# RWKV stage of a two-block kernel: the next pair's fills and key products moved from VectorE to GpSimd and ScalarE

## What is computed

```
decay = exp(-exp(-softplus(-w_raw) - 0.5))
a     = sigmoid(rw_a0 + xa @ rw_a2)
kk    = k * rw_kk, scaled to unit length over each head
k_eff = k * (1 + (a - 1) * rw_ka)
```

```
s = s * w_t + (-(s @ kk_t)) outer (kk_t * a_t) + v_t outer k_t
y_t = s @ r_t
```

## Time and profile before

| | |
|---|---|
| median of 3 runs | 3578.41 us (3572.24 to 3578.68) |
| profiled execution, its own time | 3575.68 us |
| its span | 3574.2 us |
| TensorE matmul busy | 3090.4 us (86%) |
| VectorE busy | 1488.6 us (42%) |
| ScalarE busy | 984.2 us (28%) |
| GpSimd busy | 45.5 us (1%) |

### The profile page before, as it was taken

One profiled execution on the slowest core, in us unless ns is written; L12 is line 12 of the kernel. 1 busy time (PEld: TensorE's weight loads), 2 busy tenths in 40 slices (PEclk: granted clock), 3 DMA queues, 4 the chain that ended last, 5 costly groups with the idle time before them and its releaser, 6 DMA issues. The chain is left out here.

```text
span 3574.2 us, 54419 instructions
## 1 busy us (share of the span) xinstructions
PE 3090.4 (86%) x23420; PEld 1656.0 (46%) x23420; DVE 1488.6 (42%) x3056; ACT 984.2 (28%) x1912; POOL 45.5 (1%) x65
## 2 busy tenths in 40 slices
PE   7888888887799999789995977787999899985996
PEld 3455555555655555444443322334454545542332
DVE  3677777776457567510023100003333424233122
ACT  2344344333124654510011000003324242410001
POOL 0000000000000000000000000000000000000000
PEclk9999999998799999889997999998999999996998
DMA  4212222211311221243056999982211111026997
GB/s 176 67 55 70 80 66 84 83 62 43 112 52 65 80 80 68 100 159 118 0 201 246 421 421 421 421 342 105 111 41 74 47 66 41 15 92 275 426 426 309
DMA packets 118062, 546.90 MB, mean 153 GB/s; under 512 B 32208, under 2 KB 35008, under 8 KB 82496
## 3 DMA queue, kind: packets, MB, share of 16 engines
q1 hardware_dynamic: 111776, 524.69, 38.0%
q0 software_dynamic: 3456, 12.58, 0.9%
q10 hardware_dynamic: 2592, 6.16, 0.4%
HBM read 511.74 MB, written 31.65 MB: 152 GB/s over the span
## 5 line engine op out<-in xcount | busy, mean ns | idle before, releaser
L2349 PE MATMUL mh_ps<-mh_w_ahead,xmT 128*128 128x512 f32 x768 | 336.4, 593 | 0.0
L2084 PE MATMUL ex_ps<-ex_ring,ex_xs 128*64 128x512 f32 x896 | 244.3, 634 | 53.3 <-DMA ex_ring<-expert_slabs_in 42.2
L501 PE MATMUL rw_ps<-hT,rw_w 128*128 128x512 f32 (+1 forms) x640 | 273.9, 555 | 6.6 <-PEq L63 5.8
L2349 PEld LDWEIGHTS mh_ps<-mh_w_ahead,xmT 128*128 128x128 f32 x768 | 144.7, 190 | 167.1 <-issue 165.1
L2084 PEld LDWEIGHTS ex_ps<-ex_ring,ex_xs 128*64 128x64 f32 x896 | 81.6, 146 | 205.7 <-issue 203.3
L1300 PE MATMUL sg_ps<-hTp,sg_w 128*128 128x512 f32 x384 | 171.0, 599 | 0.0
L501 PEld LDWEIGHTS rw_ps<-hT,rw_w 128*128 128x128 f32 x640 | 114.7, 198 | 86.7 <-issue 76.0
L2333 PE MATMUL mh_ps<-xmT,mh_w_ahead 128*128 128x512 f32 x256 | 124.5, 620 | 14.9 <-PEq L63 8.6
L2168 DVE TENSOR_TENSOR ex_hid<-ex_hid,ex_ps 128x512 f32<-128x512 f32 x16 | 11.0, 687 | 288.0 <-PE ex_ps L2084 288.0
L2992 PE MATMUL ge_ps<-ge_ring,ge_xs 128*64 128x512 f32 x512 | 116.0, 606 | 2.8 <-DVE ge_xs L3096 2.8
L1826 PE MATMUL se_ps<-se_w,se_mT 128*128 128x512 f32 x256 | 113.7, 601 | 5.1 <-DMA se_w<-w_out_in 5.1
(11 more groups left out here) (617 smaller groups left out, 5113.6 us busy)
## 6 DMA issues: line engine op xcount, KB each, us to landing
ex_ring<-expert_slabs_in SPq DMA_DIRECT2D x148, 1024.0 KB, 26.7
ge_ring<-expert_slabs_in SPq DMA_DIRECT2D x50, 2048.0 KB, 15.8
mh_w_ahead<-head_slabs_in SPq DMA_DIRECT2D x16, 2048.0 KB, 8.0
rw_mod_w<-mod_w_in SPq DMA_DIRECT2D x64, 384.0 KB, 4.1
ex_first<-expert_slabs_in SPq DMA_DIRECT2D x22, 1024.0 KB, 26.0
rw_mod_w<-ada_in SPq DMA_DIRECT2D x64, 256.0 KB, 3.3
sg_kern<-cum_dram SPq DMA_DIRECT2D x64, 256.0 KB, 3.2
ex_ring<-expert_slabs_in SPq DMA_DIRECT2D x7, 2048.0 KB, 13.8
```

The costliest lines, as they stand in the source:

```text
L501: mm = pe.matmul(where[j, part], w[:, k, P * j:P * j + P], tokens, start=k == 0, stop=k == KC - 1)
L2084: mm = pe.matmul(ps[halves[j], bank, :], src[:, k, halves[j]], home(g + j)[0][:, k, :], start=k == 0, stop=k == KC - 1)
L2349: mm = pe.matmul(ps[:, 4 + t, :], xmT[:, k, P * t:P * t + P], w[:, slot, k, :], start=k == 0, stop=k == KC - 1)
```

## The change

ScalarE computes the key factor `1 + (a - 1) * ka` as `a * ka + (1 - ka)` (`past_gate`, one 128x768 activation per direction) into the storage of `xb` and `low`, which `substitute` has finished with; a 128x1 VectorE instruction prepares `1 - ka`. GpSimd multiplies both by `k` and sums them (`replaced_keys`, two products of 128x768 and a sum of 128x512), then does `fill` for both directions, four products of 128x768 (with `kk * a` now among them) and one of 128x512 each, and only then clears `diag`'s padding and `xb`. `write_keys` and `fill` leave VectorE. `exponents(p, 1)` is cut into three pieces, which stand between scan steps 1, 2, 3 and 4. ScalarE's scaling of the values moves ahead of the second direction's factors.

```diff
+        past_ka = sb("rw_past_ka", [P, 1])
+        keyed = [a.rearrange("p i c -> p (i c)")[:, 0:NT] for a in (xb, low)]
...
-                for c in range(PAIRS):
+                def replaced_keys(p):
+                    pool.wait_ge(s.affine, 2 * p + 2)
+                    pool.wait_ge(s.shifted_k, p + 1)
+                    for d in range(2):
+                        pool.tensor_tensor(keyed[d], keyed[d], kc[:, :], ALU.mult).then_inc(s.keyed, 1)
+                    pool.wait_ge(s.keyed, 2 * p + 2)
+                    if p:
+                        pool.wait_ge(s.bonus_done, p)
+                    pool.tensor_tensor(ksum[:, :], keyed[0][:, CTX:NT], keyed[1][:, CTX:NT], ALU.add).then_inc(s.key_summed, 1)
...
+                def fill(p, d):
+                    rf, bf, kf = (e1, qq, ee) if d == 0 else (e1, ee, qq)
+                    u = of_dir(d)
+                    ul = slice(RW_NCH * d + RW_CC, RW_NCH * d + RW_NCH)
+                    pool.wait_ge(s.factors, 2 * p + d + 1)
+                    if p:
+                        pool.wait_ge(s.mr_kept, 6 * (p - 1) + 3 * d + 3)
+                    pool.tensor_tensor(bk[:, u, 64:P], token_cut(keyed[d]), token_cut(bf[:, :]), ALU.mult)
+                    pool.wait_ge(s.shifted_r, p + 1)
+                    pool.tensor_tensor(kr[:, ul, 64:P], token_cut(rc[:, :]), token_cut(rf[:, :], RW_CC), ALU.mult)
+                    pool.wait_ge(s.kk_done, p + 1)
+                    pool.tensor_tensor(sgs[:, d, :], kk[:, :], aas[:, d, :], ALU.mult).then_inc(s.gated_keys, 1)
+                    pool.tensor_tensor(kr[:, u, 0:64], token_cut(kk[:, :]), token_cut(kf[:, :]), ALU.mult)
+                    pool.wait_ge(s.gated_keys, 2 * p + d + 1)
+                    pool.tensor_tensor(bk[:, u, 0:64], token_cut(sgs[:, d, :]), token_cut(bf[:, :]), ALU.mult).then_inc(s.filled, 1)
+
+                for p in range(PAIRS):
+                    replaced_keys(p)
+                    fill(p, 0)
+                    fill(p, 1)
+                    clear(p)
...
+                def past_gate(p):
+                    par = pars2[:, p % 2, :]
+                    act.wait_ge(s.gates, 4 * p + 4)
+                    for d in range(2):
+                        act.activation(keyed[d], aas[:, d, :], ACT.Identity, scale=par[:, KA:KA + 1], bias=past_ka[:, 0:1]).then_inc(s.affine, 1)
...
+                    if prep:
+                        past_gate(p)
+                    if core:
                         keep_wu(c, 0)
...
+                        centre(p, 2, 0, vc[:, CTX:NT], ps[:, 1, :])
                         factors(p, 1)
                         act.activation(half[:, :, :], half[:, :, :], ACT.Exp, scale=-KAPPA).then_inc(s.halved, 1)
-                        centre(p, 2, 0, vc[:, CTX:NT], ps[:, 1, :])
...
+                    if part == 0:
+                        dve.wait_ge(s.gates, 4 * p + d + 1)
+                        if d:
+                            dve.wait_ge(s.filled, 2 * p + 1)
...
-                        dve.wait_ge(s.kk_done, p + 1)
-                        write_keys(p, 0)
                     if core:
                         keep_mr(c, 3)
-                        dve.wait_ge(s.mr_kept, 6 * c + 4)
-                    if prep:
-                        fill(p, 0)
-                        dve.wait_ge(s.filled, 2 * p + 1)
-                    if core:
                         keep_mr(c, 4)
-                    if prep:
-                        exponents(p, 1)
-                    if core:
                         keep_mr(c, 5)
...
                         scan_step(c, 1)
-                        scan_step(c, 2)
-                    if prep:
-                        write_keys(p, 1)
+                    for part in range(3):
+                        if prep:
+                            exponents(p, 1, part)
+                        if core:
+                            scan_step(c, part + 2)
                     if core:
-                        for step in range(3, 6):
-                            scan_step(c, step)
+                        scan_step(c, 5)
...
-                    if prep:
-                        fill(p, 1)
-                    if core:
                         dve.wait_ge(s.y_done, c + 1)
...
-                        dve.wait_ge(s.filled, 2 * p + 2)
                         dve.wait_ge(s.halved, p + 1)
+                        dve.wait_ge(s.key_summed, p + 1)
```

More of the change, by code:

```diff
@@ L964, in neighbours, with exponents @@
                     link(dve.scalar_tensor_tensor(dst[:, 0:n - 1], u[:, 1:n], par[:, 2 * j + 1:2 * j + 2], dst[:, 0:n - 1], ALU.mult, ALU.add))
-                def exponents(p, d):
-                    dve.wait_ge(s.gates, 4 * p + d + 1)
+                def exponents(p, d, part):
                     sg = sgs[:, d, :]
-                    link(dve.tensor_tensor_scan(qq[:, :], cst("chunk_start"), sg, 0.0, ALU.mult, ALU.add))
                     q3 = qq[:, :].rearrange("p (c t) -> p c t", t=RW_C)
-                    link(dve.tensor_scalar(half[:, d, :], q3[:, :, RW_C - 1], 0.5, None, ALU.mult))
-                    link(dve.tensor_tensor(q3, q3, free_copies(half[:, d, :], RW_C), ALU.subtract))
-                    dve.tensor_tensor(ee[:, :], qq[:, :], sg, ALU.subtract).then_inc(s.exponents, 1)
@@ L975, in write_keys @@
[L975 to L980, removed]
-                    link(dve.scalar_tensor_tensor(aa, aa, 1.0, kc[:, :], ALU.add, ALU.mult))
-                    if d == 0:
-                        dve.tensor_copy(ksum[:, :], aa[:, CTX:NT]).then_inc(s.ksum_started, 1)
-                    else:
-                        dve.wait_ge(s.ksum_started, p + 1)
-                        link(dve.tensor_tensor(ksum[:, :], ksum[:, :], aa[:, CTX:NT], ALU.add))
@@ L988, in fill @@
[L988 to L997 removed]
+                    if part == 0:
+                        dve.wait_ge(s.gates, 4 * p + d + 1)
+                        if d:
+                            dve.wait_ge(s.filled, 2 * p + 1)
+                        link(dve.tensor_tensor_scan(qq[:, :], cst("chunk_start"), sg, 0.0, ALU.mult, ALU.add))
+                    elif part == 1:
+                        link(dve.tensor_scalar(half[:, d, :], q3[:, :, RW_C - 1], 0.5, None, ALU.mult))
+                        link(dve.tensor_tensor(q3, q3, free_copies(half[:, d, :], RW_C), ALU.subtract))
+                    else:
+                        dve.tensor_tensor(ee[:, :], qq[:, :], sg, ALU.subtract).then_inc(s.exponents, 1)
@@ L1028, in _ @@
                         dve.sem_inc(s.shifted_k, 1)
-                        exponents(p, 0)
+                        for part in range(3):
+                            exponents(p, 0, part)
                     if core:
```

12 lines of the change are left out of this document (2 added, 10 removed).

## The result

The changed kernel takes **3534.03 us** (median of 4 runs, 3529.86 to 3537.26) against 3578.55 us (3572.24 to 3583.22) for the kernel before: a ratio of 0.9876, 95% interval 0.9857 to 0.9895. That is 44.5 us less, where 31 against the profiled execution (33.5 against this median) was forecast; 3545 was 11 us too high, and the range 3529 to 3563 holds it. The profiled execution took 3534.92 us, 40.8 less than the one before.

A forecast was written before the change was run, and what follows sets the result against it. The prediction took TensorE to bound the kernel, each wait that goes being nearly its own length off the time. Terms -27.2 - 8.5 + 1.4 + 0 + 3.2 = -31.1 against 3575.7 gave 3545 us, range 3529 to 3563.

The forecast's parts named there:

- Part 1: VectorE's prep work leaves the gap before `mr(4)` and `mr(5)`; both TensorE wait groups go, 14.4 + 12.8 = -27.2 us.
- Part 3: ScalarE's two extra activations ahead of `keep_wu(0)` start it 0.2 us late in seven pairs: +1.4 us.
- Part 2: In the scan, TensorE's 1.21 us wait at step 4 goes in seven pairs, fitting barely: -8.5 us.
- Part 4: The fills on GpSimd stay hidden in the pairs, the second behind ScalarE's copies: 0 us.
- x: Time of a 128x768 two-input product on GpSimd, absent from the trace and taken as 1.75 us.
- between 1 and 2 us: Sign of a right forecast: how long `near(1)` would wait for GpSimd.
- The limit: Longest GpSimd 128x768 product, 2.06 us, at which the second fill still ends before ScalarE takes up direction 1.
- Part 5: The opening turn, without core work to hide behind: second fill 4.6 later, partly hidden by 1.3 us slack, +3.2 us.
- The clock: Rival: TensorE's clock fall may go (5 us won) or come later, up to 1.5 us a pair: 3555 us, chance 0.09.
- a slower GpSimd: Rival: GpSimd's product takes about 2.4 us, costing 11 us in seven pairs and 6 in the opening: 3562 us, chance 0.13.
- the fill as bound: Rival: at 3.1 us a product the second fill makes `near(1)` 4.9 us late per pair: 3592 us, chance 0.05.
- Scan steps beside GpSimd's products: Rival: VectorE's scan steps wait for GpSimd's product under way, 6 us a pair, 43 in all: 3588 us, chance 0.04.

The follow-up runs named there:

- the values' neighbours: The changed kernel plus the second direction's exponents earlier and the values' neighbour instructions standing singly between scan steps; 3526.69 us, ratio 0.9846.

## Why the prediction was right, and what it missed

**Part 1** (-27.2) had the mechanism and too small a size. In a pair without a fall of the clock the two waits of the earlier trace rows are 4.45, and 0.29 more is won because the first matmuls of `mr(4)` now start among those of `wu(5)` instead of behind a wait: 4.74, which is 33 in seven. (`wu(0)` to `crossed_y` is 4.94 shorter in the table: 0.28 of Part 3 comes off the 4.74, and 0.48 is time that TensorE loses inside `new_part` in this one pair of before; the others lose 0.1 to 0.35 there.) The step that failed: "This is a sum over the stage and not one pair's 4.45 times seven, since in some pairs the second wait was shorter." It was shorter, 0.98 to 1.58 in place of 2.40, in the five pairs in which TensorE ran at its lower clock up to it, and there the time was lost all the same. The sum also holds the last pair's 1.04, which has no prep ahead of it and stayed.

**Part 2** (-8.5) held. 1.98 between `crossed_y` and `near(1)`, less the 0.69 that `keys(0)` gives back to ScalarE, is 1.29 a pair against 1.21. It fitted barely, as said: one block of 3.9 us in place of pieces brought the wait back.

**Part 3** (+1.4): `keep_wu(0)` starts 1.42 us behind `wu(0)` instead of 1.14, so 0.28 a pair, 0.18 of it a wait of TensorE. Right.

**Part 4** (0): x is 1.81 (taken 1.75), and `near(1)`'s wait 0.77 (1.3 expected, and "between 1 and 2 us" among the signs, which did not come). The limit was put at 2.06. With the change ScalarE takes up direction 1 at 338.41, 2.0 us behind the end of `near(1)` at 336.40, and one extra product of 1.9 still fitted; the limit is nearer to 1.81 + 2.0 / 4.67 = 2.24. That ScalarE's copies are the cover was shown twice, by the added products and by the one moved forward.

**Part 5** (+3.2) was 5.0. The slack that was to hide 1.3 of it did not: TensorE was idle for 4.4 us ahead of the first `near(1)` and came out of it at its lower clock, before and then after:

```profile
140.37:145.37 5.00, 4.67 (x56) 2.30 (x56) 1.03 (x5) 4.84 (x10) 0.00 (x0) 0.98 0.02 3
```

```profile
145.41:150.41 5.00, 5.00 (x52) 2.88 (x53) 0.00 (x0) 2.82 (x6) 1.24 (x3) 0.50 0.02 3
```

2.65 of the extra time can be had back by moving one product ahead of the factors. The last pair got 2.7 longer, which I had at zero: 0.7 is `keys(0)` waiting for ScalarE as in the other pairs; over 50 to 60 us behind its `near(1)` the clock is 0.66 in place of 0.83, and the rest was not taken apart further.

**The clock** had 0 in the sum, and "the fall may go (another 5 us won)" in a rival. The seven intervals shrank by 50.2 us, and Parts 1 to 3 as measured in one pair make 40; the other 10 are the clock and, in small part, losses like the one in `new_part`. In the profiled executions the forecast was 9.7 too high. The 6 of Part 1 and these 10 are more than that; Part 5 (1.8), the last pair (2.7) and what comes behind the stage (1.7) took 6 back. So the total came out nearer than its terms, and that part is luck.

The rivals: a slower GpSimd did not come, nor the fill as bound (three extra products made that case: 3577). Scan steps beside GpSimd's products take 0.28 each, and 0.48 to 0.52 for two, as those without it. The pairs are 96.8 to 97.2 apart, but for two, less than the 98 to 101 given.

## What to carry to other kernels

A wait that repeats costs what one undisturbed turn shows, not the sum over the stage: where the clock is low the wait looks shorter and the work ahead of it is longer by as much. Before moving work to a slower engine, find what else is late at the same place; that is its allowance (here 2.0 us a pair, against a forecast that would have allowed 1.2). And in a chain of small steps between two engines, spread foreign work in pieces no longer than the other engine's time between steps.

## What the runs showed of the hardware

**GpSimd holds small VectorE instructions.** VectorE's 128x8 `tensor_scalar` took 0.17 us in the kernel before:

```profile
342.23 0.17 DVE L1094 TENSOR_SCALAR rw_st<-rw_st 128x8 f32<-128x8 f32 x1
```

Beside GpSimd it takes 2.52, and ends with GpSimd's memsets, which only write. VectorE, then GpSimd, in the changed kernel:

```profile
334.07 2.52 DVE L1109 TENSOR_SCALAR rw_st<-rw_st 128x8 f32<-128x8 f32 x1
```

```profile
333.61 1.82 POOL L521 TENSOR_TENSOR rw_bk<-rw_sg,rw_e 128x768 f32<-128x768 f32 x1
335.36 0.31 POOL L502 MEMSET rw_diag<- 128x256 f32 x1
335.61 0.95 POOL L503 MEMSET rw_xb<- 128x1024 f32 x1
```

With that instruction folded into one that reads PSUM, nothing is held at its place (0.69), and the square with both inputs in SBUF takes 1.19 instead of 0.69, its start falling 0.6 us before the end of the product:

```profile
336.40 0.69 DVE L1109 SCALAR_TENSOR_TENSOR rw_tk<-rw_st,rw_ps 128x512 f32<-128x512 f32 x1
337.12 1.19 DVE L1112 TENSOR_TENSOR rw_kr<-rw_tk 128x512 f32<-128x512 f32 x1
```

```profile
335.94 1.81 POOL L521 TENSOR_TENSOR rw_bk<-rw_sg,rw_e 128x768 f32<-128x768 f32 x1
```

In the kernel with three extra products even one element per partition waits, to the end of the product that began at 350.92 and took 1.84; the short pauses between the extra products let the earlier ones through sooner:

```profile
345.40 1.37 DVE L1115 TENSOR_SCALAR rw_st<-rw_st 128x8 f32<-128x8 f32 x1
...
351.01 1.76 DVE L1129 TENSOR_TENSOR rw_fac<-rw_half 128x1 f32<-128x1 f32 x1
```

The Trainium skill (SBUF — State Buffer, Who interferes with whom) says that a two-port form contends with GpSimd and a form with two SBUF inputs only with GpSimd's reads, and that whoever is second is blocked fully. The traces agree: the memsets held the first and not the second; the scan steps and reductions, with an input from PSUM or a single one, run free beside it. The price is not a share of the bandwidth but the rest of what GpSimd has under way, and that can be more than one instruction: the 2.52 us reach over the rest of a product and two memsets that follow it without a pause.

**The clock falls and the place decides the price.** Over 5 us windows the granted clock goes down to 0.50, the lower of its two levels. A fall 15 to 25 us behind `near(1)` costs at most 0.4 us; one at 5 to 15 us, followed by a second, costs 1.6 in the changed kernel; right behind `near(1)`, after 6.8 us of idle TensorE, it costs 1.3 (three extra products); and behind waits of about 2 us ahead of `mr` there is one that costs up to 2.7. A change that only moved a wait (exponents earlier) made the seven intervals 3.7 us longer by it. What decides where the clock falls stays open.

**TensorE may wait for its code.** The gaps that no instruction releases (up to 1.58 us) all end 1.2 to 1.6 us behind the landing of a 16 KB block of instructions, as told under the values' neighbours. What they cost depends on the place: with the neighbours spread out `crossed_y` to `keys(0)` takes 25.2 to 25.3 us with a gap in or just ahead of `near(1)` and also in the last interval, without one, since ScalarE's copies cover it; with the gap inside `near(0)` it takes 26.5.
